# Low parts of the weights on VectorE and gates in two scaled fp16 parts, while expert coefficients are built

## Chip, core and metric

One core of a Trainium2 chip runs the whole program. The metric is the device time of one execution in microseconds. Of the kernel before there are three timed runs and one profiled execution.

## The reference, cut to what matters

Two transformer blocks follow each other on 256 tokens with 1024 features. The first block has two layers, and each ends in an expert stage ("PEER"). The change lies in these two expert stages alone:

```
q  = (t @ w_q)                                  # 8 heads, 2 halves of 128
sc = q . sub_keys                               # 128 scores per head and half
s1, i1 = top16(sc[:, :, 0]);  s2, i2 = top16(sc[:, :, 1])
top_s, pos = top16(all sums s1 + s2)            # 16 experts per head and token
eidx = i1 * 128 + i2 at pos;  gate = softmax(top_s)
hid = gelu(t . u[eidx]);  out = sum(gate * hid * v[eidx])
```

A token thus picks 8 x 16 = 128 of 16384 experts, each with a gate. The result is fp32.

## The kernel before, in words

The kernel gathers no expert rows. It computes the products of all tokens with all 128 chunks of `u` (128 experts each), multiplies the result with a dense matrix of coefficients, which is zero where a token didn't pick the expert, and multiplies that with all 128 chunks of `v`. The two products are fp32 in quality: each weight tile and each moving operand is split in a high and a low fp32r part, and `product3` (L412 to L414) issues three matmuls per block (high x high, high x low, low x high). A weight tile of 128 x 1024 goes through four stations: SyncE loads it in one of four ring slots (`ring`), ScalarE copies it rounded (`split_hi`, L400, into `ring_hi`), VectorE or GpSimd subtracts (`split_lo`, L406, into `ring_lo`), TensorE uses it. SyncE's load of tile n waits for the low part of tile n - 4. `split_lo` waits on the semaphore `hi_ready` for the high part of the same tile.

Each expert stage is ten segments (`SEGMENTS`). Segments 1 and 5, the two coefficient stages of a layer, are the ones of kind "upcoef": 16 items each, four items to a loop iteration. Segment 0 does `u` alone ("up"), the others do `u` and `v` ("pair") or `v` ("down").

An item j of a coefficient stage has on each engine, in this order:

- TensorE: the first 12 matmuls of the up product; the coefficients of eight tokens (`coefficients`, L689), in two batches of four tokens; the other 12 matmuls of the up product; the coefficients of another eight tokens, again in two batches. The coefficients of a token are a product of one-hots: a stationary one-hot of the second key (128 x 128) with the gated one-hot of the first key (128 x 64), once for each of the three bf16 parts of the gate. A batch is thus 12 matmuls, an item 48.
- ScalarE: `split_hi` of the tile two items ahead (`AHEAD = 2`), then `store_coef` (L988) for the first eight tokens, `gelu` (L983) of the up product, and `store_coef` (L988) for the second eight tokens. Each of the last three waits for TensorE's bank. The engine takes them in this order, so `split_hi` of item j comes behind the last `store_coef` of item j - 1.
- VectorE: for each of the four batches, three instructions, first key compared (L1394, 256 elements), second key compared (L1395, 512 elements) and gated (L1398, 768 elements). There are buffers for four batches, so VectorE may be up to four batches ahead of TensorE; it waits on `hots_read` and on `bank_done` of earlier batches, and on nothing of ScalarE.
- GpSimd: `split_lo` of the tile two items ahead.

Which engine takes `split_lo` is set by the lists `POOL_SLOTS`: GpSimd has the tiles from the query stage up to segment 2, and those of segment 5 with its two tiles of lead; VectorE has the others. Before segment 1 VectorE turns the gates into the parts by a chain of copies and subtractions (`peer`, L1375 and L1378) from `gate_rest`, which ScalarE fills at L996.

Of the kernel before, what the change touches and what calls it, by code (L numbers as in the profile page):

```python
# [16 lines left out]
ALU = mybir.AluOpType  # L17
# [1 line left out]
AX = mybir.AxisListType  # L19
F32 = mybir.dt.float32  # L20
F32R = mybir.dt.float32r
BF16 = mybir.dt.bfloat16
U32 = mybir.dt.uint32

P = 128
D = 1024
K = D // P
# [4 lines left out]
ALL = slice(0, TA)  # L32
NT = S // P
EPS = 1e-6
NEG = -1e30
HEADS = 4
RING = 4
# [142 lines left out]

POOL_SLOTS = []
for _l in range(2):
    POOL_SLOTS += [range(SLOT0[f"query{_l}"] + AHEAD, SLOT0[f"expert{_l}.2"]),
                   range(SLOT0[f"expert{_l}.5"] + AHEAD, SLOT0[f"expert{_l}.6"] + AHEAD)]


HEAD_SLOTS = range(SLOT0["mix"] + AHEAD, SLOT0["mix"] + QK2)
# [25 lines left out]
def build(nc, a):  # L213
    with ExitStack() as ctx:
        def sb(name, shape, dt=F32):
            return ctx.enter_context(nc.sbuf_tensor(name, shape, dt))
# [17 lines left out]
        sub_keys = desk[:, 0:16 * NKEYS].rearrange("p (h e) -> p h e", e=NKEYS)  # L234


        rows = desk[:, :].bitcast(BF16).rearrange("p (b e t) -> p b e t", b=3, t=4)
        last = product[:, :, :].rearrange("p b t -> p (b t)").bitcast(BF16).rearrange("p (e t) -> p e t", t=4)
        hot_second = [rows[:, b, 0:P, :] for b in range(3)] + [rstd[:, 0:2 * P].bitcast(BF16).rearrange("p (e t) -> p e t", t=4)]
        hot_first = [rows[:, b, P:P + HALF, :] for b in range(3)] + [last[:, 0:HALF, :]]  # L240
        hot_gated = [x.rearrange("p (x e) t -> p x e t", x=3) for x in [rows[:, b, P + HALF:, :] for b in range(3)] + [last[:, HALF:, :]]]
        weighed = sb("weighed", [P, 2, 4, S], F32R)

        picks = sb("picks", [P, 5, S], BF16)
        gate_rest = rstd[:, 0:S]
        keys4 = sb("keys4", [P, NKEYS, 4], BF16)
        small = sb("small", [P, 16])


# [219 lines left out]
        def _(pool):  # L469
            pool.memset(eps_col, EPS).then_inc(memset_done, 1)  # L470
            for x, slots in enumerate(POOL_SLOTS):
                if x % 2 == 0:

                    pool.wait_ge(normed_ready, K * (x + 2))
                    pool.dma_start(desk[:, 0:16 * NKEYS], a[f"subkey{x // 2}"]).then_inc(keys_in, 16)

                pool.wait_ge(lo_ready, slots[0])
                with pool.Fori(0, len(slots) // RING) as i:
                    for q in range(RING):
                        split_lo(pool, slots[q], i)  # L480
                for n in slots[len(slots) - len(slots) % RING:]:
                    split_lo(pool, n)
# [27 lines left out]
        def _(pe):  # L510
# [128 lines left out]
            def peer(l):  # L639
# [40 lines left out]
                def coefficients(w, count, i=0, step=3):  # L680

                    pe.wait_ge(bank_free[w % 4], i * step + w // 4)
                    for b in range(2):
                        pe.wait_ge(hots_ready, i * 16 + (2 * count + b + 1))
                        for t in range(4):
                            y = 4 * b + t
                            for x in range(3):
                                at = (2 * count + b) % 4
                                mm = pe.matmul(work[:, w % 4, y * HALF:(y + 1) * HALF], hot_second[at][:, :, t], hot_gated[at][:, x, :, t], start=(x == 0), stop=(x == 2))  # L689
                        mm.then_inc(*((hots_read, 1) if b == 0 else (bank_done[w % 4], 1)))  # L690

                built = l * 2 * S // 8
# [177 lines left out]
        def _(act):  # L870
# [89 lines left out]
            def peer(l):  # L960
# [24 lines left out]

                def store_coef(w, at, i=0, step=3):
                    act.wait_ge(bank_done[w % 4], i * step + (w // 4 + 1))
                    act.activation(arena[:, bass.ds(i * (64 * HALF) + (HELD * S + at * HALF), 8 * HALF)], work[:, w % 4, :], ACT.Copy).then_inc(bank_free[w % 4], 1)  # L988

                for x, (kind, e, h, steps) in enumerate(SEGMENTS):  # L990
                    if x == 1:
                        gate_exp(1)
                        for t in range(NT):
                            w = W0[f"turn{l}"] + t
                            act.wait_ge(*done(w))
                            act.activation(gate_rest[:, t * P:(t + 1) * P], work[:, w % 4, 2 * P:3 * P], ACT.Copy)  # L996
                            act.activation(picks[:, 0:2, t * P:(t + 1) * P], work[:, w % 4, 0:2 * P].rearrange("p (x q) -> p x q", x=2), ACT.Copy).then_inc(bank_free[w % 4], 1)
                    w0, base, slots, step = W0[f"expert{l}.{x}"], SLOT0[f"expert{l}.{x}"], SLOTS_OF[kind], ITEMS_OF[kind]
                    if kind == "upcoef" and x > 1:
# [138 lines left out]
        def _(dve):  # L1138
# [230 lines left out]
            def peer(l):  # L1369
                split_to(SLOT0[f"query{l}"])  # L1370
                choose(l)
                for t in range(NT):
                    dve.wait_ge(*freed(W0[f"turn{l}"] + t))
                for x in range(2, 5):
                    dve.tensor_copy(picks[:, x, :], gate_rest).then_inc(vec.sem, vec.up())  # L1375
                    step()
                    if x < 4:
                        dve.tensor_tensor(gate_rest, gate_rest, picks[:, x, :], ALU.subtract).then_inc(vec.sem, vec.up())  # L1378
                        step()
                c0 = l * CHUNKS  # L1380

                def one_hots(count, tok, h0, w, i, pace=3):

                    for b in range(2):

                        if w is not None:
                            if b == 0:
                                dve.wait_ge(hots_read, i * 8 + (count - 1))
                            else:
                                dve.wait_ge(bank_done[w % 4], i * pace + (w // 4 + 1))  # L1390
                        of = lambda x, n: picks[:, x:x + n, bass.ds(i * 64 + (tok + 4 * b), 4)]
                        at = (2 * count + b) % 4
                        first, second = hot_first[at], hot_second[at]
                        dve.tensor_tensor(first, keys4[:, h0:h0 + HALF, :], of(0, 1).to_broadcast([P, HALF, 4]), ALU.is_equal).then_inc(hots_used, 1)  # L1394
                        dve.tensor_tensor(second, keys4[:, :, :], of(1, 1).to_broadcast([P, P, 4]), ALU.is_equal)  # L1395
                        dve.wait_ge(hots_used, i * 16 + (2 * count + b + 1))
                        shape = [P, 3, HALF, 4]
                        dve.tensor_tensor(hot_gated[at], first.unsqueeze(1).to_broadcast(shape), of(2, 3).unsqueeze(2).to_broadcast(shape), ALU.mult).then_inc(hots_ready, 1)  # L1398

                def weigh(e, i):  # L1400

# [15 lines left out]
                for x, (kind, e, h, steps) in enumerate(SEGMENTS):  # L1417
# [1 line left out]
                        continue  # L1419
                    w0, base, slots, pace = W0[f"expert{l}.{x}"], SLOT0[f"expert{l}.{x}"], SLOTS_OF[kind], ITEMS_OF[kind]  # L1420
                    h0 = 0 if x == 1 else HALF
                    if x == 2:
                        dve.wait_ge(lo_ready, base)
                        ahead[0] = base
                        split_to(base - 1)
                    if x == 6:
                        dve.wait_ge(lo_ready, base + AHEAD)
                    if x in (2, 6):

# [12 lines left out]
                    def four(at, i):  # L1442
                        for j in range(at, at + 4):
                            if e is not None:
                                weigh(e + j, i)
                            if kind != "upcoef":
                                for y in range(slots):
                                    n = base + j * slots + AHEAD + y
                                    split_lo(dve, n, i, 4 * slots)
                            if kind == "upcoef":  # L1450
                                for y in range(2):
                                    w = w0 + pace * (j - 1) + 1 + y if j else None
# [268 lines left out]
```

## Time and profile before

| what | value |
|---|---|
| median of 3 runs | 2897.3 us (2894.17 to 2898.11) |
| span of the profiled execution | 2891.4 us |
| its own time beside the span | not listed apart; the runs lie 2.8 to 6.7 us above the span |
| TensorE busy | 2729.4 us, 94% |
| VectorE busy | 2039.1 us, 71% |
| ScalarE busy | 1176.0 us, 41% |
| GpSimd busy | 471.9 us, 16% |
| mean granted TensorE clock | 0.955 of full |
| `split_lo` on VectorE / on GpSimd | 647 of 1217 ns / 152 of 3029 ns |

The span is the time from the first to the last instruction. A row of the timeline reads: start and duration in us, engine, line, operation, written tile, read tiles, shapes, count, and in brackets the idle time before it with what ended it. L689 is the coefficients' matmul, L412 to L414 the three matmuls of `product3`, and the granted clock is 1.00 at full speed (2.4 GHz) and 0.50 at half (1.2 GHz).

### The profile page before, as it was taken

How to read it: one execution, taken by the hardware profiler on the slowest of the kernel's cores; microseconds unless marked ns; L12 is line 12 of the kernel's file. 1: busy time of each engine (PE TensorE's matmuls, PEld its weight loads, DVE VectorE, ACT ScalarE, POOL GpSimd, SP SyncE). 2: the span in 40 equal slices, each digit the busy share in tenths (PEclk: the TensorE clock that was granted, in tenths of full speed). 3: DMA queues.
4: the chain of work that ended last, by engine and by line, in shares of the span. 5: the costliest groups of instructions: out<-in, count | busy, mean ns of one | idle time of the engine just before them, and what ended most of it. 6: DMA issues, size and time to landing. Idle time of an engine off the chain costs nothing. (4 is left out here: it accounts for less than half of the span.)

```text
span 2891.4 us, 60103 instructions
## 1 busy us (share of the span) xinstructions
PE 2729.4 (94%) x23064; PEld 2634.6 (91%) x23064; DVE 2039.1 (71%) x3796; ACT 1176.0 (41%) x1706; POOL 471.9 (16%) x174
## 2 busy tenths in 40 slices
PE   8799699999999999996999999999989988999999
PEld 7799699999999999896999999999989987559998
DVE  6559996667996787599976668966875546346663
ACT  4444344444344434453444443444343344234432
POOL 0038450000340000175600001600000022000000
PEclk9899899999999999998999999999999999559999
DMA  5244225555335554443255554255535543405454
GB/s 192 94 148 158 89 87 193 185 185 186 117 117 185 186 186 149 164 163 104 80 175 182 184 187 146 87 189 184 187 124 176 167 131 110 61 22 172 161 184 148
DMA packets 120738, 429.61 MB, mean 149 GB/s; under 512 B 14714, under 2 KB 16762, under 8 KB 120200
## 3 DMA queue, kind: packets, MB, share of 16 engines
q1 hardware_dynamic: 118464, 420.65, 43.6%
q0 software_dynamic: 2128, 7.00, 1.4%
q8 instruction: 94, 1.54, 0.2%
q14 instruction: 52, 0.43, 0.0%
HBM read 423.85 MB, written 3.74 MB: 148 GB/s over the span
## 5 line engine op out<-in xcount | busy, mean ns | idle before, releaser
L406 DVE TENSOR_TENSOR ring_lo<-ring,ring_hi 128x1024 fp32r<-128x1024 f32 (+1 forms) x647 | 784.6, 1217 | 515.7 <-ACT ring_hi L400 514.7
L412 PE MATMUL work<-normed_hi,ring_hi 128*128 128x256 f32 (+1 forms) x3728 | 1078.1, 289 | 47.6 <-DVE normed_lo L1175 27.6
L413 PE MATMUL work<-normed_lo,ring_hi 128*128 128x256 f32 (+1 forms) x3728 | 1067.3, 286 | 0.0
L414 PE MATMUL work<-normed_hi,ring_lo 128*128 128x256 f32 (+1 forms) x3728 | 1058.7, 284 | 0.0
L400 ACT ACTIVATE ring_hi<-ring 128x1024 fp32r<-128x1024 f32 (+1 forms) x799 | 830.7, 1051 | 543.7 <-PE acc L414 384.8
L412 PEld LDWEIGHTS work<-normed_hi,ring_hi 128*128 128x128 f32 x3728 | 719.7, 193 | 54.6 <-issue 35.6
L413 PEld LDWEIGHTS work<-normed_lo,ring_hi 128*128 128x128 f32 x3728 | 715.1, 192 | 0.8
L414 PEld LDWEIGHTS work<-normed_hi,ring_lo 128*128 128x128 f32 x3728 | 715.3, 192 | 0.0
L406 POOL TENSOR_TENSOR ring_lo<-ring,ring_hi 128x1024 fp32r<-128x1024 f32 x152 | 459.5, 3029 | 930.3 <-ACT ring_hi L400 930.0
L413 PE MATMUL acc<-weighed,ring_hi 128*128 128x256 f32 x2048 | 576.3, 281 | 0.0
L412 PE MATMUL acc<-weighed,ring_hi 128*128 128x256 f32 x2048 | 576.0, 281 | 0.0
L414 PE MATMUL acc<-weighed,ring_lo 128*128 128x256 f32 x2048 | 575.6, 281 | 0.0
L414 PEld LDWEIGHTS acc<-weighed,ring_lo 128*128 128x128 f32 x2048 | 386.6, 189 | 0.0
L413 PEld LDWEIGHTS acc<-weighed,ring_hi 128*128 128x128 f32 x2048 | 386.4, 189 | 0.0
L412 PEld LDWEIGHTS acc<-weighed,ring_hi 128*128 128x128 f32 x2048 | 386.3, 189 | 0.0
L983 ACT ACTIVATE arena<-work 128x256 f32 (+1 forms) x256 | 98.5, 385 | 397.4 <-PE work L414 397.3
L904 ACT ACTIVATE arena<-work 128x256 f32<-128x256 f32 (+4 forms) x168 | 68.6, 408 | 345.4 <-PE work L414 279.0
L689 PE MATMUL work<-desk 128*128 128x64 bf16 x2304 | 165.2, 242 | 11.3 <-DVE desk L1398 11.2
L1410 DVE TENSOR_TENSOR product<-arena 128x256 f32 (+1 forms) x256 | 158.7, 620 | 9.9 <-ACT arena L988 9.9
L689 PEld LDWEIGHTS work<-desk 128*128 128x128 bf16 x2304 | 141.7, 118 | 20.3 <-DVE desk L1398 15.6
L988 ACT ACTIVATE arena<-work 128x512 f32 (+1 forms) x128 | 76.6, 598 | 189.1 <-PE work L689 189.1
L1398 DVE TENSOR_TENSOR desk<-desk,picks 128x768 bf16<-128x768 bf16 x192 | 140.8, 734 | 0.0
(187 smaller groups left out, 2607.8 us busy)
## 6 DMA issues: line engine op xcount, KB each, us to landing
ring<-in_u SPq DMA_DIRECT2D x256, 512.0 KB, 3.2
ring<-in_v SPq DMA_DIRECT2D x256, 512.0 KB, 3.2
ring<-in_ffn_in SPq DMA_DIRECT2D x88, 512.0 KB, 3.3
ring<-in_query SPq DMA_DIRECT2D x32, 512.0 KB, 3.3
ring<-in_ffn_out SPq DMA_DIRECT2D x32, 512.0 KB, 4.4
ring<-in_even_in SPq DMA_DIRECT2D x28, 512.0 KB, 4.2
ring<-in_odd_in SPq DMA_DIRECT2D x24, 512.0 KB, 3.2
ring<-in_mix_in SPq DMA_DIRECT2D x19, 512.0 KB, 3.2
```

The source lines that it names most:

```text
L400: act.activation(ring_hi[:, n % RING, 0:width], ring[:, n % RING, 0:width], ACT.Copy).then_inc(hi_ready, 1)
L406: eng.tensor_tensor(ring_lo[:, n % RING, 0:width], ring[:, n % RING, 0:width], ring_hi[:, n % RING, 0:width].bitcast(F32), ALU.subtract).t ...
L412: pe.matmul(out, w_hi, hi, start=start, stop=False, **more)
L413: pe.matmul(out, w_hi, lo, start=False, stop=False, **more)
L414: return pe.matmul(out, w_lo, hi, start=False, stop=stop, **more)
L689: mm = pe.matmul(work[:, w % 4, y * HALF:(y + 1) * HALF], hot_second[at][:, :, t], hot_gated[at][:, x, :, t], start=(x == 0), stop=(x == 2))
L904: act.activation(dst, src, func).then_inc(bank_free[w % 4], 1)
L983: act.activation(hidden[:, bass.ds(i * 4 + h % HELD, 1), :].squeeze(1) if not isinstance(i, int) else hidden[:, h % HELD, :], work[:, w % ...
L988: act.activation(arena[:, bass.ds(i * (64 * HALF) + (HELD * S + at * HALF), 8 * HALF)], work[:, w % 4, :], ACT.Copy).then_inc(bank_free[w ...
L1398: dve.tensor_tensor(hot_gated[at], first.unsqueeze(1).to_broadcast(shape), of(2, 3).unsqueeze(2).to_broadcast(shape), ALU.mult).then_inc(h ...
L1410: dve.tensor_tensor(product[:, e % 2, :], hid, co, ALU.mult).then_inc(coef_read, 1)
```

## The change

Five edits go together.

1. GpSimd's list ends two tiles into segment 1 of each layer (`POOL_SLOTS` has one range per layer, not two). In segments 1 and 5 `split_lo` is VectorE's; in the order of the code it stands ahead of the item's one-hots.
2. The one-hots, the gates and the keys are fp16 instead of bf16.
3. A gate has two parts instead of three. ScalarE multiplies it by 2^15 when it fills `gate_rest`, and by 2^-15 when it stores the coefficients.
4. So the gated instruction writes 512 elements instead of 768, and TensorE has 8 matmuls per batch instead of 12. The chain ahead of segment 1 has one copy and one subtraction instead of three copies and two subtractions.
5. At segment 1 VectorE waits for GpSimd's last low part (`lo_ready`, `base + AHEAD`); the wait and the two low parts that VectorE formed ahead of segment 2, and the wait ahead of segment 6, are gone.

```diff
--- before.py
+++ after.py
@@ -19,7 +19,7 @@
 AX = mybir.AxisListType
 F32 = mybir.dt.float32
 F32R = mybir.dt.float32r
-BF16 = mybir.dt.bfloat16
+F16 = mybir.dt.float16
 U32 = mybir.dt.uint32
 
 P = 128
@@ -32,6 +32,7 @@
 ALL = slice(0, TA)
 NT = S // P
 EPS = 1e-6
+GATE_SCALE = 2.0 ** 15
 NEG = -1e30
 HEADS = 4
 RING = 4
@@ -180,8 +181,7 @@
 
 POOL_SLOTS = []
 for _l in range(2):
-    POOL_SLOTS += [range(SLOT0[f"query{_l}"] + AHEAD, SLOT0[f"expert{_l}.2"]),
-                   range(SLOT0[f"expert{_l}.5"] + AHEAD, SLOT0[f"expert{_l}.6"] + AHEAD)]
+    POOL_SLOTS.append(range(SLOT0[f"query{_l}"] + AHEAD, SLOT0[f"expert{_l}.1"] + AHEAD))
 
 
 HEAD_SLOTS = range(SLOT0["mix"] + AHEAD, SLOT0["mix"] + QK2)
@@ -234,16 +234,16 @@
         sub_keys = desk[:, 0:16 * NKEYS].rearrange("p (h e) -> p h e", e=NKEYS)
 
 
-        rows = desk[:, :].bitcast(BF16).rearrange("p (b e t) -> p b e t", b=3, t=4)
-        last = product[:, :, :].rearrange("p b t -> p (b t)").bitcast(BF16).rearrange("p (e t) -> p e t", t=4)
-        hot_second = [rows[:, b, 0:P, :] for b in range(3)] + [rstd[:, 0:2 * P].bitcast(BF16).rearrange("p (e t) -> p e t", t=4)]
+        rows = desk[:, :].bitcast(F16).rearrange("p (b e t) -> p b e t", b=3, t=4)
+        last = product[:, :, :].rearrange("p b t -> p (b t)").bitcast(F16).rearrange("p (e t) -> p e t", t=4)
+        hot_second = [rows[:, b, 0:P, :] for b in range(3)] + [rstd[:, 0:2 * P].bitcast(F16).rearrange("p (e t) -> p e t", t=4)]
         hot_first = [rows[:, b, P:P + HALF, :] for b in range(3)] + [last[:, 0:HALF, :]]
-        hot_gated = [x.rearrange("p (x e) t -> p x e t", x=3) for x in [rows[:, b, P + HALF:, :] for b in range(3)] + [last[:, HALF:, :]]]
+        hot_gated = [x.rearrange("p (x e) t -> p x e t", x=2) for x in [rows[:, b, P + HALF:P + 3 * HALF, :] for b in range(3)] + [last[:, HALF:3 * HALF, :]]]
         weighed = sb("weighed", [P, 2, 4, S], F32R)
 
-        picks = sb("picks", [P, 5, S], BF16)
+        picks = sb("picks", [P, 4, S], F16)
         gate_rest = rstd[:, 0:S]
-        keys4 = sb("keys4", [P, NKEYS, 4], BF16)
+        keys4 = sb("keys4", [P, NKEYS, 4], F16)
         small = sb("small", [P, 16])
 
 
@@ -469,10 +469,8 @@
         def _(pool):
             pool.memset(eps_col, EPS).then_inc(memset_done, 1)
             for x, slots in enumerate(POOL_SLOTS):
-                if x % 2 == 0:
-
-                    pool.wait_ge(normed_ready, K * (x + 2))
-                    pool.dma_start(desk[:, 0:16 * NKEYS], a[f"subkey{x // 2}"]).then_inc(keys_in, 16)
+                pool.wait_ge(normed_ready, K * (2 * x + 2))
+                pool.dma_start(desk[:, 0:16 * NKEYS], a[f"subkey{x}"]).then_inc(keys_in, 16)
 
                 pool.wait_ge(lo_ready, slots[0])
                 with pool.Fori(0, len(slots) // RING) as i:
@@ -684,9 +682,9 @@
                         pe.wait_ge(hots_ready, i * 16 + (2 * count + b + 1))
                         for t in range(4):
                             y = 4 * b + t
-                            for x in range(3):
+                            for x in range(2):
                                 at = (2 * count + b) % 4
-                                mm = pe.matmul(work[:, w % 4, y * HALF:(y + 1) * HALF], hot_second[at][:, :, t], hot_gated[at][:, x, :, t], start=(x == 0), stop=(x == 2))
+                                mm = pe.matmul(work[:, w % 4, y * HALF:(y + 1) * HALF], hot_second[at][:, :, t], hot_gated[at][:, x, :, t], start=(x == 0), stop=(x == 1))
                         mm.then_inc(*((hots_read, 1) if b == 0 else (bank_done[w % 4], 1)))
 
                 built = l * 2 * S // 8
@@ -985,7 +983,7 @@
 
                 def store_coef(w, at, i=0, step=3):
                     act.wait_ge(bank_done[w % 4], i * step + (w // 4 + 1))
-                    act.activation(arena[:, bass.ds(i * (64 * HALF) + (HELD * S + at * HALF), 8 * HALF)], work[:, w % 4, :], ACT.Copy).then_inc(bank_free[w % 4], 1)
+                    act.activation(arena[:, bass.ds(i * (64 * HALF) + (HELD * S + at * HALF), 8 * HALF)], work[:, w % 4, :], ACT.Copy, scale=1.0 / GATE_SCALE).then_inc(bank_free[w % 4], 1)
 
                 for x, (kind, e, h, steps) in enumerate(SEGMENTS):
                     if x == 1:
@@ -993,7 +991,7 @@
                         for t in range(NT):
                             w = W0[f"turn{l}"] + t
                             act.wait_ge(*done(w))
-                            act.activation(gate_rest[:, t * P:(t + 1) * P], work[:, w % 4, 2 * P:3 * P], ACT.Copy)
+                            act.activation(gate_rest[:, t * P:(t + 1) * P], work[:, w % 4, 2 * P:3 * P], ACT.Copy, scale=GATE_SCALE)
                             act.activation(picks[:, 0:2, t * P:(t + 1) * P], work[:, w % 4, 0:2 * P].rearrange("p (x q) -> p x q", x=2), ACT.Copy).then_inc(bank_free[w % 4], 1)
                     w0, base, slots, step = W0[f"expert{l}.{x}"], SLOT0[f"expert{l}.{x}"], SLOTS_OF[kind], ITEMS_OF[kind]
                     if kind == "upcoef" and x > 1:
@@ -1371,12 +1369,10 @@
                 choose(l)
                 for t in range(NT):
                     dve.wait_ge(*freed(W0[f"turn{l}"] + t))
-                for x in range(2, 5):
-                    dve.tensor_copy(picks[:, x, :], gate_rest).then_inc(vec.sem, vec.up())
-                    step()
-                    if x < 4:
-                        dve.tensor_tensor(gate_rest, gate_rest, picks[:, x, :], ALU.subtract).then_inc(vec.sem, vec.up())
-                        step()
+                dve.tensor_copy(picks[:, 2, :], gate_rest).then_inc(vec.sem, vec.up())
+                step()
+                dve.tensor_tensor(picks[:, 3, :], gate_rest, picks[:, 2, :], ALU.subtract).then_inc(vec.sem, vec.up())
+                step()
                 c0 = l * CHUNKS
 
                 def one_hots(count, tok, h0, w, i, pace=3):
@@ -1394,8 +1390,8 @@
                         dve.tensor_tensor(first, keys4[:, h0:h0 + HALF, :], of(0, 1).to_broadcast([P, HALF, 4]), ALU.is_equal).then_inc(hots_used, 1)
                         dve.tensor_tensor(second, keys4[:, :, :], of(1, 1).to_broadcast([P, P, 4]), ALU.is_equal)
                         dve.wait_ge(hots_used, i * 16 + (2 * count + b + 1))
-                        shape = [P, 3, HALF, 4]
-                        dve.tensor_tensor(hot_gated[at], first.unsqueeze(1).to_broadcast(shape), of(2, 3).unsqueeze(2).to_broadcast(shape), ALU.mult).then_inc(hots_ready, 1)
+                        shape = [P, 2, HALF, 4]
+                        dve.tensor_tensor(hot_gated[at], first.unsqueeze(1).to_broadcast(shape), of(2, 2).unsqueeze(2).to_broadcast(shape), ALU.mult).then_inc(hots_ready, 1)
 
                 def weigh(e, i):
 
@@ -1419,11 +1415,7 @@
                         continue
                     w0, base, slots, pace = W0[f"expert{l}.{x}"], SLOT0[f"expert{l}.{x}"], SLOTS_OF[kind], ITEMS_OF[kind]
                     h0 = 0 if x == 1 else HALF
-                    if x == 2:
-                        dve.wait_ge(lo_ready, base)
-                        ahead[0] = base
-                        split_to(base - 1)
-                    if x == 6:
+                    if x == 1:
                         dve.wait_ge(lo_ready, base + AHEAD)
                     if x in (2, 6):
 
@@ -1443,10 +1435,9 @@
                         for j in range(at, at + 4):
                             if e is not None:
                                 weigh(e + j, i)
-                            if kind != "upcoef":
-                                for y in range(slots):
-                                    n = base + j * slots + AHEAD + y
-                                    split_lo(dve, n, i, 4 * slots)
+                            for y in range(slots):
+                                n = base + j * slots + AHEAD + y
+                                split_lo(dve, n, i, 4 * slots)
                             if kind == "upcoef":
                                 for y in range(2):
                                     w = w0 + pace * (j - 1) + 1 + y if j else None
```

## Rows read from the trace of the kernel before

**Rows 1.** The page: span, and each engine's busy time, share and instructions.

```profile
span 2891.4 us, 60103 instructions
...
PE 2729.4 (94%) x23064; PEld 2634.6 (91%) x23064; DVE 2039.1 (71%) x3796; ACT 1176.0 (41%) x1706; POOL 471.9 (16%) x174
```

**Rows 2.** Busy time by stretch, the four coefficient stages; columns as named.

```profile
core 0: us, PE busy (x) PEld busy (x) DVE busy (x) ACT busy (x) POOL busy (x), PEclk, DMA share, GB/s
338.29:430.17 91.88, 90.40 (x1082) 87.62 (x1082) 86.88 (x174) 37.99 (x60) 48.22 (x13) 1.00 0.24 82
...
sum 368.70, PE 362.08 PEld 350.49 DVE 350.20 ACT 151.95 POOL 208.89; mean PE 90.52 PEld 87.62 DVE 87.55 ACT 37.99 POOL 52.22
```

**Rows 3.** Timeline of TensorE inside the first coefficient stage.

```profile
346.98 0.36 PE L412 MATMUL work<-normed_hi,ring_hi 128*128 128x256 f32 x1
...
348.49 0.92 PE L689 MATMUL work<-desk 128*128 128x64 bf16 x12
349.22 0.91 PE L689 MATMUL work<-product,rstd 128*128 128x64 bf16 x12
349.94 0.36 PE L412 MATMUL work<-normed_hi,ring_hi 128*128 128x256 f32 x1
```

**Rows 4.** Timeline of ScalarE inside the first coefficient stage.

```profile
350.17 0.60 ACT L988 ACTIVATE arena<-work 128x512 f32<-128x512 f32 x1 [1.10 <-PE work L689]
350.67 1.05 ACT L400 ACTIVATE ring_hi<-ring 128x1024 fp32r<-128x1024 f32 x1
...
356.07 0.60 ACT L988 ACTIVATE arena<-work 128x512 f32<-128x512 f32 x1 [1.11 <-PE work L689]
```

**Rows 5.** Timeline of VectorE, one split and the one-hots behind it.

```profile
743.92 1.22 DVE L406 TENSOR_TENSOR ring_lo<-ring,ring_hi 128x1024 fp32r<-128x1024 f32 x1 [0.20 <-ACT ring_hi L400]
745.06 0.28 DVE L1394 TENSOR_TENSOR desk<-keys,picks 128x256 bf16<-128x256 bf16 x1
745.26 0.42 DVE L1395 TENSOR_TENSOR desk<-keys,picks 128x512 bf16<-128x512 bf16 x1
745.60 0.55 DVE L1398 TENSOR_TENSOR desk<-desk,picks 128x768 bf16<-128x768 bf16 x1
746.07 0.28 DVE L1394 TENSOR_TENSOR desk<-keys,picks 128x256 bf16<-128x256 bf16 x1
```

**Rows 6.** Timeline of VectorE where GpSimd works beside it.

```profile
388.49 2.75 DVE L1398 TENSOR_TENSOR desk<-desk,picks 128x768 bf16<-128x768 bf16 x1
```

**Rows 7.** Timeline of TensorE behind that instruction.

```profile
391.30 0.91 PE L689 MATMUL work<-desk 128*128 128x64 bf16 x12 [0.34 <-DVE desk L1398]
```

**Rows 8.** Timeline of GpSimd, first coefficient stage.

```profile
327.98 2.36 POOL L406 TENSOR_TENSOR ring_lo<-ring,ring_hi 128x1024 fp32r<-128x1024 f32 x1 [20.34 <-ACT ring_hi L400]
...
388.30 2.52 POOL L406 TENSOR_TENSOR ring_lo<-ring,ring_hi 128x1024 fp32r<-128x1024 f32 x1 [0.21 <-ACT ring_hi L400]
```

**Rows 9.** Timeline of VectorE at the start of the stage.

```profile
327.39 0.42 DVE L1378 TENSOR_TENSOR rstd<-rstd,picks 128x256 f32<-128x256 f32 x1
```

**Rows 10.** Timeline of TensorE at the start of the stage, at half clock.

```profile
332.14 1.93 PE L689 MATMUL work<-desk 128*128 128x64 bf16 x24 [3.22 <-DVE desk L1398]
333.88 0.56 PE L412 MATMUL work<-normed_hi,ring_hi 128*128 128x256 f32 x1
...
336.59 0.93 PE L689 MATMUL work<-desk 128*128 128x64 bf16 x12
```

**Rows 11.** Busy time by stretch around idle times of TensorE; columns as before.

```profile
306.80:309.30 2.50, 0.00 (x0) 0.00 (x0) 2.40 (x9) 2.21 (x5) 0.84 (x1) 1.00 0.56 192
309.40:325.40 16.00, 0.00 (x0) 0.00 (x0) 15.57 (x13) 0.00 (x0) 0.00 (x0) 0.50 0.06 22
...
1364.10:1367.40 3.30, 3.11 (x31) 2.95 (x32) 3.30 (x12) 1.24 (x2) 0.00 (x0) 0.50 0.28 109
2427.50:2430.30 2.80, 0.00 (x0) 0.00 (x0) 2.76 (x3) 1.38 (x4) 0.00 (x0) 1.00 0.58 187
2430.30:2435.00 4.70, 4.67 (x38) 4.62 (x39) 4.46 (x5) 2.65 (x4) 0.00 (x0) 1.00 0.34 112
```

## The prediction

> **What bounds the kernel now.** I read the page's busy times first: TensorE is busy 94% of a span of 2891.4 us, VectorE 71% [rows 1]. So a stage gains only where TensorE waits or has less to do. Next I read the busy times by stretch. From the last coefficient store of item 0 to that of item 15 the four coefficient stages take 91.88 us (the first) and 368.70 us together. That is 60 intervals of 6.145 us, in which TensorE is busy 362.08 us at full clock and VectorE 350.20 us [rows 2]: both are near their limit. Then the timelines. TensorE does 12 coefficient matmuls in 0.73 us (349.22 - 348.49, next 349.94 - 349.22 = 0.72), 0.0605 us each, and half an up product in 348.49 - 346.98 = 1.51 us [rows 3]. An undisturbed item takes 356.07 - 350.17 = 5.90 us from last store to last store [rows 4]. Items that take more have a VectorE instruction stretched: gating took 2.75 us instead of 0.55 [rows 5, 6], a GpSimd subtraction started at 388.30 beside it [rows 8], and TensorE sat idle 0.34 us until it ended [rows 7].
>
> **The order decides.** ScalarE starts the next high part 0.50 us after it starts the item's last store: 350.17, 350.67 [rows 4]. That store waits for TensorE to end the item. Before, GpSimd alone waited for this high part. Now VectorE waits for it, and behind that wait in VectorE's queue stand the split and all four batches of the same item, and for these TensorE waits. VectorE can no longer be a batch ahead: each item becomes a chain through three engines.
>
> From the start of the last store, step by step:
> - to the start of the high part 0.50, the high part 1.05 [rows 4], handed over 0.05 (GpSimd took 0.08: 350.67 + 1.05 = 351.72 to its start 351.80, a VectorE start I take as a little faster, and it is small);
> - split to first comparison 745.06 - 743.92 = 1.14, to the second 0.20, to the gating 0.34 [rows 5]; the gating of 512 elements I take as the 512-element comparison, 0.42 [rows 5]. Batch 0 is ready after 3.70 us.
> - Batch 1 is ready one batch later. A batch takes 746.07 - 745.06 = 1.01 now [rows 5]; the 768-element instruction holds 0.47 of that, one of 512 holds 0.34 (745.60 - 745.26), so it becomes 0.88.
> - TensorE starts 0.06 after the gating ends (388.49 + 2.75 = 391.24, 391.30 [rows 6, 7]). Then 8 matmuls, 0.485; half the up product, 1.51; batches 2 and 3, ready by now, 16 x 0.0605 = 0.97; and 0.22 to the start of the store (349.22 + 0.73 = 349.95, 350.17 [rows 3, 4]). Together 3.25.
>
> The new interval is 3.70 + 0.88 + 3.25 = 7.83 us. The first half of the up product lies inside the 3.70 and is hidden; TensorE then idles some 2.4 us per item (free about 1.3 after the store's start, resumed at 3.76). VectorE's own work is 1.14 + 4 x 0.88 = 4.66, no limit. 60 x 7.83 = 469.8, against 368.7: **+101.1 us**.
>
> **What is gained.** The matmuls that go, 16 per item, are worth 0.97 us each item and are in the sum already. At the start of each layer's first stage the chain of parts is shorter: the subtraction ends at 327.39 + 0.42 = 327.81 [rows 9], the split can start where GpSimd's did, 327.98 [rows 8], batch 0 is ready at 330.08 and TensorE starts at 330.14 instead of 332.14 [rows 10]. At the half clock there, batch 1 starts at 331.02, takes 8 x 0.0725 (24 took 333.88 - 332.14 = 1.74) = 0.58, the half product 336.59 - 333.88 = 2.71 [rows 10], 16 matmuls 1.16, tail 0.22: store at 335.69 instead of 338.29, -2.6 us, twice. In item 0 of each second stage the high part is issued while TensorE still has a chunk and half a product to do (2.8 + 1.5 us, from three and a half products' worth of 1.4 to 1.5), more than the chain's 3.2 from its release: no wait, 16 matmuls less, -0.97, twice. Together **-7.2 us**.
>
> **Edits at nothing.** The new wait at segment 1 is for low parts that GpSimd forms before 327.98 [rows 8]; VectorE arrives at 327.8 and its own split waits for the high part released at the same moment. The two low parts ahead of segment 2 go: they stood under the last items' TensorE work, and if that cover were not there they would give back 2 x 1.14 us, twice a layer at most. ScalarE's scale factors change no shape: a handful of instructions per layer outside the chain, and 128 stores inside it, where between nothing and a doubling of 0.60 [rows 4] I take nothing, since size and engine stay. No DMA is moved; a load waits for the low part four tiles earlier, two items before its use. fp16 matmuls and comparisons are not in this trace. They have the bytes of bf16, which excludes a gain; if a matmul cost as much as one of a 256-column up product (1.51 / 12 = 0.126 instead of 0.0605), 24 in the chain would add 1.6 us per item, 94 us. I take the bf16 row, the nearest, and keep a little of the other end.
>
> **The clock.** The chain gives TensorE an idle of about 2.4 us 60 times. What do the rows say of that? After 306.80 TensorE did nothing, the clock was still 1.00 for 2.5 us and then 0.50 [rows 11]: so 2.4 to 2.5 us of idle can be enough. But an idle of 2.86 us from 2427.48 kept 1.00, before and behind it [rows 11]. In the trace every idle at full clock above 3.3 us ended in a fall, and none of up to 1.66 did. So in some items the clock falls, in others not. Once fallen, it stayed at 0.50 at least for a stretch like 1364.10 to 1367.40, with TensorE busy 3.11 of 3.30 us [rows 11], and at the start of the stage it stayed there through an idle of 3.22 us [rows 10]. A fall at the end of the idle costs, with such a short stretch, some 1.9 us of up product at 2.71 / 1.51 of its time, 0.83, and 0.1 for matmuls, 0.9; if it lasts the item, 2.71 - 1.51 = 1.20 for the half product and 24 x 0.012 = 0.29, together 1.49. I take 1.2. How often lies between never (0) and always (60 x 1.49 = +89.4). With one row on each side half would be the plain choice; I take 0.6, since one idle follows another every 8 us and a fall can outlast an item. 60 x 0.6 x 1.2 = **+43.2 us**.
>
> The Trainium skill (TensorE: Matmul & The Clock Gate, "HAM oscillation") says that a loop that waits on every pass can fall to the lower clock again on each. This trace shows single falls only; by the rule the sum would lean to the upper end.
>
> **The sum.** +101.1 - 7.2 + 43.2 = +137.1 us. The span of 2891.4 becomes 3028.5; the runs lie 2.8 to 6.7 us above the span, so on the median of 2897.3 the forecast is 3034 us.
>
> **The rivals.**
> - *The clock stays full.* For it speaks the idle of 2.86 us; against it 306.80. +93.9, 2991 us.
> - *The clock is half in all these items.* Against it: TensorE is then busy most of each item, and busy stretches brought it back [rows 11]. 101.1 - 7.2 + 89.4 = +183.3, 3081 us.
> - *Faster: the split waits for nothing.* The case with the other sign. What now stretches VectorE (2.75 for 0.55) goes with GpSimd's subtractions, and if high parts were there in time, TensorE alone would set the item: 5.90 - 0.97 = 4.93, above VectorE's 4.66. 60 x (4.93 - 6.145) = -72.9, with -7.2 it is -80.1, 2817 us. It decides at one point: whether the high part is written before TensorE ends the item before. Against it is ScalarE's order, seen in the rows as 0.50 us between the two starts.
> - *A partial loss.* Some release that I see as serial overlaps; between 2890 and 2970.
>
> The Trainium skill (GPSIMD Engine Reference, "Key points") says that GpSimd shares its SBUF interfaces with VectorE and contends with instructions that read two SBUF inputs. By that rule alone the change gains what the third rival says. The trace agrees on the contention: 2.75 us instead of 0.55 [rows 6, 5].
>
> **How the numbers follow.** Forecast 0.58, clock full 0.18, clock half 0.14, faster 0.07, partial 0.03. The range is to reach from a little under the full-clock case to the half-clock case: 2978 to 3082 us. Faster by over 0.2%: 0.07. Within 0.2% (about what a measurement of this kernel can tell from no change): 0.01. Slower: 0.58 + 0.18 + 0.14 + 0.02 = 0.92.
>
> **What would show it.** Last store to last store 7.8 to 9.3 us; VectorE's split in these stages 0.05 us behind the high part, idle time of VectorE ended by ScalarE's high part about 60 x 3 us; TensorE idle some 2.4 us before the first batch of each item, ended by VectorE's gating; GpSimd with 92 subtractions (2 x 40 + 12) and none stretched by one-hots; no VectorE one-hot above 0.5 us; granted clock below 1.00 in parts of these stages. I am wrong if VectorE's one-hots run ahead of TensorE, if items take 5 us, or if the time outside these four stages moves by more than a few us.

## The result and the profile after

The changed kernel takes 3036.99 us (median of 4 runs, 3031.82 to 3043.34) against 2895.74 us (4 runs of before): 1.0492 times as long, 95% interval 1.0477 to 1.0508. The profiled execution has a span of 3036.3 us, 144.9 us above that of before.

The page of the changed kernel, as [rows 1] of before:

```profile
span 3036.3 us, 58005 instructions
...
PE 2739.5 (90%) x22040; PEld 2628.2 (87%) x22040; DVE 1956.9 (64%) x3850; ACT 1175.5 (39%) x1706; POOL 249.2 (8%) x114
```

Every engine's share fell. TensorE has 1024 matmuls less and is busy 10 us longer: part of its work ran at half clock. The four coefficient stages, last store of item 0 to last store of item 15, as [rows 2]:

```profile
core 0: us, PE busy (x) PEld busy (x) DVE busy (x) ACT busy (x) POOL busy (x), PEclk, DMA share, GB/s
336.07:465.89 129.82, 92.90 (x842) 86.15 (x842) 70.81 (x195) 37.91 (x60) 0.00 (x0) 0.83 0.17 61
789.13:920.22 131.09, 94.81 (x842) 88.01 (x842) 70.76 (x195) 37.93 (x60) 0.00 (x0) 0.80 0.17 60
...
sum 522.85, PE 378.05 PEld 350.74 DVE 283.11 ACT 151.68 POOL 0.00; mean PE 94.51 PEld 87.69 DVE 70.78 ACT 37.92 POOL 0.00
```

They grew from 368.70 to 522.85 us, by 154.2 us, to 8.714 us per item instead of 6.145; all the rest of the program became 9.2 us shorter. VectorE is busy 283.11 of 522.85 us there and GpSimd not at all: no engine is short of time, they wait for each other. One item on each engine follows, ScalarE, VectorE, TensorE (as [rows 4, 5, 7]). In the changed kernel L986 is `store_coef`, L981 the gelu, L400 and L406 the two splits, L1390, L1391 and L1394 the three one-hot instructions and L687 the coefficients' matmul; in the variants below some of these lie a few lines off:

```profile
406.85 0.60 ACT L986 ACTIVATE arena<-work 128x512 f32 x1 [0.58 <-PE work L687]
407.34 1.05 ACT L400 ACTIVATE ring_hi<-ring 128x1024 fp32r<-128x1024 f32 x1
412.25 0.60 ACT L986 ACTIVATE arena<-work 128x512 f32 x1 [3.86 <-PE work L687]
...
414.71 0.60 ACT L986 ACTIVATE arena<-work 128x512 f32 x1 [0.60 <-PE work L687]
```

```profile
408.42 1.22 DVE L406 TENSOR_TENSOR ring_lo<-ring,ring_hi 128x1024 fp32r<-128x1024 f32 x1 [4.21 <-ACT ring_hi L400]
409.56 0.28 DVE L1390 TENSOR_TENSOR desk<-keys,picks 128x256 f16<-128x256 f16 x1
409.77 0.42 DVE L1391 TENSOR_TENSOR desk<-keys,picks 128x512 f16<-128x512 f16 x1
410.10 0.42 DVE L1394 TENSOR_TENSOR desk<-desk,picks 128x512 f16<-128x512 f16 x1
410.44 0.29 DVE L1390 TENSOR_TENSOR desk<-keys,picks 128x256 f16<-128x256 f16 x1
```

```profile
410.58 0.66 PE L687 MATMUL work<-desk 128*128 128x64 f16 x8 [2.34 <-DVE desk L1394]
411.45 0.67 PE L687 MATMUL work<-desk 128*128 128x64 f16 x8 [0.21 <-DVE desk L1394]
413.43 0.66 PE L687 MATMUL work<-desk 128*128 128x64 f16 x8
```

Read the starts as a relay: store 406.85, high part 407.34, split 408.42, comparison 409.56, gating 410.10 to 410.52, matmul 410.58. The split was idle for 4.21 us until the high part came, TensorE for 2.34 us until the gating ended. This item took 414.71 - 406.85 = 7.86 us, at full clock. Most took more:

```profile
371.27:380.38 9.11, 7.19 (x58) 6.71 (x58) 4.72 (x13) 2.52 (x4) 0.00 (x0) 0.75 0.16 58
406.85:414.71 7.86, 5.31 (x59) 4.89 (x57) 4.72 (x13) 2.52 (x4) 0.00 (x0) 1.00 0.18 67
```

VectorE and ScalarE do exactly the same in both items (4.72 and 2.52 us); TensorE needs 7.19 instead of 5.31 us, at a mean granted clock of 0.75 of full, which is a mix of the two levels 2.4 and 1.2 GHz. Of 60 intervals 52 lie above 8.0 us, and each of them holds some half clock; the other 8 hold none and take 7.75 to 7.87.

### The profile page after: what moved, and what is told of

It reads as the page before. It is cut to its first block and busy times, and to the rows that moved or that the text cites. A ratio compares the mean times of both kernels' runs of the same rounds, so it can differ in the third digit from the quotient of the medians.

```text
span 3036.3 us, 58005 instructions
## 1 busy us (share of the span) xinstructions
PE 2739.5 (90%) x22040; PEld 2628.2 (87%) x22040; DVE 1956.9 (64%) x3850; ACT 1175.5 (39%) x1706; POOL 249.2 (8%) x114
## 5 line engine op out<-in xcount | busy, mean ns | idle before, releaser
L406 DVE TENSOR_TENSOR ring_lo<-ring,ring_hi 128x1024 fp32r<-128x1024 f32 x707 | 858.4, 1218 | 757.1 <-ACT ring_hi L400 756.0
L412 PE MATMUL work<-normed_hi,ring_hi 128*128 128x256 f32 (+1 forms) x3728 | 1104.7, 296 | 47.8 <-DVE normed_lo L1173 27.6
L414 PE MATMUL work<-normed_hi,ring_lo 128*128 128x256 f32 (+1 forms) x3728 | 1082.9, 290 | 0.0
L400 ACT ACTIVATE ring_hi<-ring 128x1024 fp32r<-128x1024 f32 (+1 forms) x799 | 830.4, 1051 | 542.7 <-PE acc L414 384.8
L412 PEld LDWEIGHTS work<-normed_hi,ring_hi 128*128 128x128 f32 x3728 | 744.6, 200 | 54.9 <-issue 35.7
L413 PEld LDWEIGHTS work<-normed_lo,ring_hi 128*128 128x128 f32 x3728 | 740.9, 199 | 0.8
L414 PEld LDWEIGHTS work<-normed_hi,ring_lo 128*128 128x128 f32 x3728 | 740.5, 199 | 0.0
L981 ACT ACTIVATE arena<-work 128x256 f32 (+1 forms) x256 | 98.5, 385 | 448.2 <-PE work L414 448.1
L687 PE MATMUL work<-desk 128*128 128x64 f16 x1536 | 128.5, 242 | 147.7 <-DVE desk L1394 147.7
L687 PEld LDWEIGHTS work<-desk 128*128 128x128 f16 x1536 | 95.2, 123 | 176.3 <-DVE desk L1394 171.2
L406 POOL TENSOR_TENSOR ring_lo<-ring,ring_hi 128x1024 fp32r<-128x1024 f32 x92 | 236.8, 2584 | 79.0 <-ACT ring_hi L400 78.8
L986 ACT ACTIVATE arena<-work 128x512 f32 (+1 forms) x128 | 76.5, 598 | 282.9 <-PE work L687 282.9
L412 PE MATMUL work<-arena_parts,ring_hi 128*128 128x256 f32 (+1 forms) x480 | 136.6, 285 | 4.4 <-DVE arena_parts L1157 4.4
```

What stands on the lines that cost most here:

```text
L400: act.activation(ring_hi[:, n % RING, 0:width], ring[:, n % RING, 0:width], ACT.Copy).then_inc(hi_ready, 1)
L406: eng.tensor_tensor(ring_lo[:, n % RING, 0:width], ring[:, n % RING, 0:width], ring_hi[:, n % RING, 0:width].bitcast(F32), ALU.subtract).t ...
L412: pe.matmul(out, w_hi, hi, start=start, stop=False, **more)
L413: pe.matmul(out, w_hi, lo, start=False, stop=False, **more)
L414: return pe.matmul(out, w_lo, hi, start=False, stop=stop, **more)
L981: act.activation(hidden[:, bass.ds(i * 4 + h % HELD, 1), :].squeeze(1) if not isinstance(i, int) else hidden[:, h % HELD, :], work[:, w % ...
```

## Experiments

Each was compared with the kernel before on the same chip (medians of before: 2895.7 us beside the changed kernel, 2894.1 beside e1 to e4, 2895.9 beside e5 to e8, so times of different rows may be off against each other by some 2 us). e7 and e8 have two timed runs each, the others four. The table has the kernels; below it each stands with its edit and its expectation. "Interval" is the mean over the 60 in the profiled execution.

| kernel | median us | ratio to before (95%) | interval us |
|---|---|---|---|
| changed | 3036.99 | 1.0492 (1.0477 to 1.0508) | 8.714 |
| e1, low part behind the one-hots | 2810.88 | 0.9712 (0.9692 to 0.9732) | 4.947 |
| e2, gates alone | 2854.84 | 0.9859 (0.9836 to 0.9882) | 5.647 |
| e3, low part on VectorE alone | 3119.32 | 1.0781 (1.0758 to 1.0805) | 9.96 |
| e4, changed with 10 filler matmuls | 2992.43 | 1.0348 (1.0322 to 1.0374) | 7.846 |
| e5, e1's order, three bf16 parts | 2876.27 | 0.9937 (0.9920 to 0.9953) | 5.934 |
| e6, high part ahead of the last store | 2925.79 | 1.0103 (1.0085 to 1.0121) | 6.826 |
| e7, 5 filler matmuls | 3003.47 | 1.0374 (1.0348 to 1.0401) | 8.093 |
| e8, 2 filler matmuls | 3012.13 | 1.0404 (1.0382 to 1.0426) | 8.166 |

**e1: is it the order?**

```diff
-                            for y in range(slots):
-                                n = base + j * slots + AHEAD + y
-                                split_lo(dve, n, i, 4 * slots)
                             if kind == "upcoef":
                                 ... (one_hots, twice)
+                            for y in range(slots):
+                                n = base + j * slots + AHEAD + y
+                                split_lo(dve, n, i, 4 * slots)
```

> The changed kernel with one edit: in the coefficient stages VectorE forms the low part behind the item's one-hots instead of ahead of them. Theory (order): the one-hots run ahead of TensorE again, since nothing of them stands behind the wait for the high part. TensorE alone sets the item, 5.90 - 0.97 = 4.93 us, VectorE's work is 4.66, the clock stays full, 60 intervals are 296 us instead of 523, and the time is about 2815 us (2800 to 2840). Rival (load): VectorE has too much to do once the split is its own, or fp16 operands are dearer; then the order changes little, items stay above 7 us and the time above 2950.

Measured 2810.88 us, 226 us below the changed kernel, from three lines moved. The stages in e1:

```profile
333.52:407.75 74.23, 74.23 (x842) 72.95 (x842) 70.02 (x194) 37.97 (x60) 0.00 (x0) 1.00 0.34 110
...
sum 296.85, PE 296.85 PEld 291.74 DVE 277.95 ACT 151.93 POOL 0.00; mean PE 74.21 PEld 72.93 DVE 69.49 ACT 37.98 POOL 0.00
```

TensorE has no idle time left, 4.947 us per item against the 4.93 of the theory. VectorE does the same 3850 instructions as in the changed kernel (277.95 and 283.11 us in these stages), so load is refuted as the cause. How it looks on VectorE in e1:

```profile
384.61 1.23 DVE L406 TENSOR_TENSOR ring_lo<-ring,ring_hi 128x1024 fp32r<-128x1024 f32 x1 [0.22 <-ACT ring_hi L400]
385.75 0.28 DVE L1390 TENSOR_TENSOR desk<-keys,picks 128x256 f16<-128x256 f16 x1
```

The same split waits 0.22 us instead of 4.21, since four batches of one-hots stand ahead of it.

**e2: the gates alone.** The changed kernel with `POOL_SLOTS` and the waits of before:

```diff
-    POOL_SLOTS.append(range(SLOT0[f"query{_l}"] + AHEAD, SLOT0[f"expert{_l}.1"] + AHEAD))
+    POOL_SLOTS += [range(SLOT0[f"query{_l}"] + AHEAD, SLOT0[f"expert{_l}.2"]),
+                   range(SLOT0[f"expert{_l}.5"] + AHEAD, SLOT0[f"expert{_l}.6"] + AHEAD)]
```

> The gate edits alone (two scaled fp16 parts, 8 matmuls per batch), with the low parts on GpSimd as in the kernel before. Theory (order): nothing waits for the high part, so no loss. VectorE's work is 4 x 0.88 = 3.52 us per item and each GpSimd subtraction holds it up by about 2.2 us, as before: 5.72 us per item, 60 x (5.72 - 6.145) = -25 us, with 3 to 8 us at the starts about 2866 us. Rival (fp16): if the two parts or the scaling cost time themselves, this kernel is slower than the one before, 2900 or more.

Measured 2854.84 us, 39 below its before (28 expected). The fp16 rival is refuted: comparisons of fp16 take 0.28 and 0.42 us, the values of bf16 [rows 5], and e1's 4.947 us per item are what the price of bf16 matmuls gave (4.93). What holds up VectorE in e2 is GpSimd, as before:

```profile
380.06 0.42 DVE L1397 TENSOR_TENSOR desk<-desk,picks 128x512 f16<-128x512 f16 x1
380.42 2.47 DVE L1393 TENSOR_TENSOR desk<-keys,picks 128x256 f16<-128x256 f16 x1
382.81 2.61 DVE L1394 TENSOR_TENSOR desk<-keys,picks 128x512 f16<-128x512 f16 x1
385.34 0.41 DVE L1397 TENSOR_TENSOR desk<-desk,picks 128x512 f16<-128x512 f16 x1
```

The expectation left something out: the clock fell in e2 too, to a mean of 0.96 to 0.98 in the four stages, where it is 1.00 in the kernel before [rows 2]. It fell seven times, once behind an idle of TensorE of 3.16 us and else behind idles of only 1.0 to 1.3 us. One of these on TensorE, and the stretch from 1.5 us after its end:

```profile
397.20 0.66 PE L690 MATMUL work<-desk 128*128 128x64 f16 x8 [1.02 <-DVE desk L1397]
```

```profile
398.70:401.90 3.20, 3.20 (x22) 3.11 (x22) 3.03 (x11) 1.54 (x2) 1.42 (x1) 0.50 0.15 60
```

**e3: the low part alone.** The kernel before with the other half of the change, the order included, and three bf16 parts:

```diff
-                            if kind != "upcoef":
-                                for y in range(slots):
+                            for y in range(slots):
```

> The low parts on VectorE ahead of the one-hots alone, with three bf16 parts as in the kernel before. Theory (order): the same chain as in the changed kernel, longer by the third part: 0.13 in the first gating, 0.13 in the second batch, 24 chain matmuls grow by 12 x 0.0605 = 0.73; 7.86 + 0.99 = 8.85 us per item at full clock, 60 x (8.85 - 6.145) = +162, and the falls of the clock on top at about 0.85 per item, +51: about 3105 us (3050 to 3140). Rival (fp16): the loss comes from the gates, and this kernel stays near 2896.

Measured 3119.32 us, the sign and the size of the theory, 14 us above it. The loss is this half's alone. Two intervals hold no half clock, 8.78 and 8.88 us (8.85 expected); the other 58 are at 9.50 to 10.38. Against a mean of 9.955 the falls cost 1.1 us per interval, more than the 0.85 that I carried over.

```profile
338.56:486.58 148.02, 109.57 (x1082) 102.71 (x1082) 78.76 (x195) 37.94 (x60) 0.00 (x0) 0.83 0.16 53
```

**e4: does the clock cost what it seems to?** TensorE gets more to do in its idle time:

```diff
-                def coefficients(w, count, i=0, step=3):
+                def coefficients(w, count, i=0, step=3, fill=0):
 
                     pe.wait_ge(bank_free[w % 4], i * step + w // 4)
+                    flat = keys4[:, :, :].rearrange("p e t -> p (e t)")
+                    for _ in range(fill):
+                        pe.matmul(work[:, w % 4, :], flat[:, 0:P], flat, start=True, stop=True)
```

with `fill=10` in the call inside an up product.

> The changed kernel with work added: ahead of the first batch's wait in each item TensorE does 10 matmuls of 512 columns from a constant tile into the bank that the coefficients overwrite. They take 2.1 us at full clock and lie in the idle of 2.4 us. Theory (clock): the granted clock stays at 1.00 in the four stages, items take 7.9 us, 51 us of half clock go, and the two or three us that fillers cost in each stage's item 0, where TensorE doesn't idle as long, come back: about 2995 us, 40 less than the changed kernel although it does more. Rival (the chain alone is longer than thought, the clock's fall costs nothing): the same 3037 us or more, with items still at 8.7.

Measured 2992.43 us, 44.6 us less than the changed kernel with 640 matmuls more. The stages:

```profile
336.89:454.59 117.70, 111.47 (x993) 86.05 (x992) 70.84 (x195) 37.93 (x61) 0.00 (x0) 1.00 0.20 67
...
sum 470.78, PE 445.86 PEld 344.13 DVE 283.14 ACT 151.73 POOL 0.00; mean PE 111.46 PEld 86.03 DVE 70.79 ACT 37.93 POOL 0.00
```

The clock is 1.00, the interval 7.846 us, which is also where the 8 full-clock intervals of the changed kernel lie. That measures both parts of the loss apart: the chain at full clock is 470.78 us, and the falls add 522.85 - 470.78 = 52.1.

**e5: and GpSimd's part in the kernel before?** e3 with e1's order. Its edit is that of e1.

> The low part behind the one-hots on VectorE, with three bf16 parts: the kernel before with GpSimd's subtractions in the coefficient stages moved to VectorE and nothing else. Theory: TensorE's 48 coefficient matmuls set the item at 5.90 us, VectorE's 4.03 + 1.14 = 5.17 lies under it, and what GpSimd cost VectorE before (intervals of 6.5 us among those of 5.9) is gone: 60 x (5.92 - 6.145) = -14, about 2881 us with full clock. Rival: the stretched VectorE instructions have another cause than GpSimd's subtraction; then intervals of 6.5 stay and the time is 2896 or, with the split on top, more.

Measured 2876.27 us, 19.6 below its before (14 expected). Intervals of 5.90 to 6.05 us nearly throughout; those of 6.5 are gone:

```profile
749.15:838.08 88.93, 88.93 (x1082) 87.67 (x1082) 77.32 (x187) 38.06 (x61) 0.00 (x0) 1.00 0.27 89
```

VectorE's time for these stages is 310.57 us with the splits and was 350.20 without them [rows 2]: what GpSimd's subtractions stretched was more than the splits cost. In the kernel before 56 one-hot instructions of these stages took 1.6 to 2.8 us, in e5 none took more than 0.56.

In stage time the move of the low parts is worth 368.70 - 356.03 = 12.7 us with three gate parts, but 338.80 (e2) - 296.85 (e1) = 42.0 us with two. With three parts GpSimd's subtractions stretch items from 5.9 us, where TensorE sets them, to some 6.5; with two parts TensorE alone would need 4.9, and the stretched items of e2 still take some 6.4.

**e6: shorten the chain at its other end.** VectorE's order stays that of the change; ScalarE forms the next item's high part earlier:

```diff
+                                if not last or j < at + 3:
+                                    split_hi(act, base + j + 1 + AHEAD, i, 4, step)
                                 store_coef(w0 + step * j + 2, 16 * j + 8, i)
```

(`split_hi` at the head of the item goes, except at item 0; the last four items stand behind the loop.)

> The changed kernel, with VectorE's order kept and ScalarE's changed instead: it forms the high part of the next item behind the gelu and ahead of the item's last store, so some 1 us of TensorE's coefficients no longer stands ahead of it. Theory (order): the chain begins at the gelu's start: 0.28 to the high part, 1.05, 0.05, 1.14, 0.96 to batch 0, 0.06, then 0.88, 0.485 and 1.51, and 0.04 to the next gelu: 6.45 us per item. TensorE's idle falls to about 1.2 us and the clock stays full. 60 x (6.45 - 8.71) = -136: about 2900 us, near the kernel before (2885 to 2915). Rival (load): moving one ScalarE instruction does nothing, 3037.

Measured 2925.79 us, 111 us less than the changed kernel: the load rival is refuted, but the theory promised 2900. The chain in numbers, ScalarE in e6:

```profile
367.25 0.38 ACT L981 ACTIVATE arena<-work 128x256 f32 x1 [0.89 <-PE work L414]
367.53 1.05 ACT L400 ACTIVATE ring_hi<-ring 128x1024 fp32r<-128x1024 f32 x1
368.48 0.59 ACT L986 ACTIVATE arena<-work 128x512 f32 x1
```

and TensorE, first batch:

```profile
370.77 0.66 PE L687 MATMUL work<-desk 128*128 128x64 f16 x8 [1.20 <-DVE desk L1402]
```

From gelu to first matmul it is 3.52 us (3.54 expected). The way back to the next gelu is 373.97 - 370.77 = 3.20 instead of 2.92: I had left out that the last up matmul has some 0.25 us to run before the gelu may start. The 45 intervals without half clock take 6.63 us on average instead of 6.45. And 11 of the 60 are at 7.27 to 7.99, although TensorE idles only some 1.2 us: there the clock fell, which I had excluded.

**e7 and e8: how much idle time is too much?** e4 with `fill=5` and with `fill=2`.

> As the run with 10 filler matmuls, with 5 (1.07 us), which leaves TensorE an idle of 1.3 us per item. Theory (idle time decides on the clock, and idles up to 1.66 us never cost it): clock at 1.00, items of 7.85 us, about 2990 us. Rival (every wait in the item costs the clock something): between 2992 and 3037.

> The same with 2 fillers (0.43 us), idle of about 2.0 us per item. No row shows which way 2.0 goes: longer than the 1.66 that never cost the clock, shorter than 2.4 which cost it in 52 of 60 items. If falls grow evenly between, half as many as in the changed kernel: about 3012 us. If idle below 2.4 is harmless, 2990.

e8 came out at 3012.13 as expected, e7 at 3003.47 and not at 2990. With an idle of 1.2 to 1.3 us the clock still fell. TensorE in e7, an idle and the stretches around it:

```profile
362.19 0.66 PE L690 MATMUL work<-desk 128*128 128x64 f16 x8 [1.22 <-DVE desk L1397]
```

```profile
361.00:362.10 1.10, 0.00 (x0) 0.00 (x0) 1.10 (x5) 0.00 (x0) 0.00 (x0) 1.00 0.00 0
362.20:364.30 2.10, 1.88 (x22) 1.71 (x23) 2.10 (x8) 0.44 (x1) 0.00 (x0) 1.00 0.72 250
364.90:368.00 3.10, 3.10 (x27) 3.01 (x27) 0.00 (x0) 1.51 (x3) 0.00 (x0) 0.53 0.00 0
368.20:370.00 1.80, 1.67 (x10) 0.78 (x9) 1.54 (x3) 0.23 (x1) 0.00 (x0) 1.00 0.00 0
```

The idle before the first batch is 1.22 us. For some 2 us behind it TensorE works at full clock; then the granted clock is half for some 3 us and full again. 23 of 60 intervals are above 8.0 us in e7, 25 in e8, 52 in the changed kernel, none in e4. The expectation of e7 is refuted, and that e8 hit its number was luck: falls do not grow evenly with the idle, or e7 would have had next to none.

The length of one idle doesn't decide, and neither does its coming back: in the kernel before six idles of 1.24 to 1.45 us followed each other, one every 5 us, and the clock stayed full. The stretch, and one of the idles:

```profile
2397.00:2424.00 27.00, 18.77 (x137) 17.32 (x137) 19.16 (x12) 12.37 (x24) 12.09 (x6) 1.00 0.33 108
```

```profile
2413.37 0.67 PE L762 MATMUL work<-arena,const 128*128 128x256 f32 x2 [1.45 <-ACT arena L1070]
```

In the coefficient stages the idle is followed by two short batches of 64-column matmuls with another gap of 0.2 us between; there it is followed by matmuls of 256 or 272 columns. What exactly the chip weighs these runs don't separate, and it stays open.

## Why the prediction was right, step by step

The forecast was 3034 us, measured 3036.99; by spans +137.1 forecast, +144.9 measured. That a sum hits so closely has a part of luck: its second term was a guess between 0 and 89.4 us and is off by 8.9. The terms:

| term | forecast us | measured us |
|---|---|---|
| chain at full clock, 60 intervals | 7.83 each, +101.1 | 7.846 each (e4), +102.08 |
| half clock in the stages | +43.2 | +52.07 |
| outside the intervals | -7.2 | -9.20 |
| sum | +137.1 | +144.95 |

- **The order decides: right.** Each link is in the rows: 0.49, 1.08 with the hand-over, 1.14, 0.21, 0.33, 0.42, 0.06, and from the first matmul to the next store 4.13 (4.07 forecast). e1 shows it: with the same instructions in the other order the loss is not only gone, it is a gain.
- **VectorE's own work is no limit: right.** 4.66 us forecast per item, 4.72 measured as busy time. It waited for the high part 60 times, 4.0 us each and not 3, because the items took 8.7 us.
- **fp16 costs what bf16 costs: right** (e2, and eight matmuls follow in 0.485 us or less). The other bound, 94 us, was far off.
- **The clock: right in kind, both its factors wrong, and they made up for each other in part.** I forecast falls in 0.6 of the items at 1.2 us. Half clock came in 52 of 60 (0.87), and cost 52.1 / 52 = 1.0 us each. Within the rows I had (2.5 us enough once, 2.86 us not enough once) the share was a guess. One row it leaned on, that no idle of up to 1.66 us ended in a fall, is true of the kernel before and doesn't carry over to this item, as e2, e6 and e7 show.
- **Outside the intervals: right in sign, short by 2 us, with the parts unlike the forecast.** In the first layer the first copy of the gate chain to the last store of item 0 took 338.29 - 327.06 = 11.23 us and takes 336.07 - 328.91 = 7.16, 4.1 less and not 2.6: I had taken half clock for the whole of item 0, and its second half product ran at full clock, 1.5 instead of 2.7 us. In the second layer it was at half clock, as forecast, and 10.70 us became 8.44, 2.3 less. From the last store of segment 1 to that of item 0 of segment 5 the layers gave 1.0 and 2.2 us (0.97 forecast for each); why the second gave more isn't shown.
- **The rivals.** Full clock (2991) is what e4 gives, 2992. Half clock in all items (3081) is out. "Faster, the split waits for nothing" (2817) fell for this kernel and came true for e1, 2811: its price was right and its condition, that the high part be there in time, is exactly what the order denied. The Trainium skill (GPSIMD Engine Reference, "Key points") says that GpSimd contends for the SBUF interfaces with VectorE instructions that read two SBUF inputs. The traces agree: one-hots of 2.5 us beside GpSimd's subtraction in e2, none above 0.43 us in the changed kernel, where GpSimd is idle in these stages. By that rule the change gains, and e1 has that gain; the wait that came with it here cost 173.9 us at full clock, more than the 42.0 us that the move itself is worth with two gate parts (e2 to e1).

So the change has three effects, in stage time: the order at full clock 470.78 - 296.85 = +173.9 us, the clock +52.1, and the intended part 296.85 - 368.70 = -71.9. How the intended part divides depends on which half comes first: the move off GpSimd gives 12.7 us and then the third gate part 59.2 (by e5), or the third gate part 29.9 us and then the move 42.0 (by e2, with the clock's falls in e2 in it).

The best version is e1: 2810.88 us, 2.9% below the kernel before and 7.4% below the changed one.

## What to carry to other kernels

When work moves to another engine, look first at what it waits for and what stands behind it in the new queue; its own duration comes second. Here 1.14 us of work, free of cost behind the one-hots, cost 2.9 us per item at full clock ahead of them, because the wait for its input tied three engines in a ring. And price a new idle time of TensorE twice, once as time and once as clock: filling it with useless matmuls gave 45 us back.

## What I had not expected of the hardware

Idle times of only 1.0 to 1.3 us were enough to bring the granted clock to half now and then: 11 (e6) and 23 (e7) of 60 intervals were visibly longer for it, and in e2 it fell six times behind such idles. In the kernel before longer ones, up to 1.66 us, never did that. 2 fillers (0.43 us) already halved the number of long intervals, 52 to 25, and 3 more did little, to 23; only the full cover took it to 0. The half clock doesn't begin with the idle: in e7's rows it came some 2 us after TensorE was at work again.
